# Expert stage of a hybrid decoder step: gathers of four slots for 32 tokens, a value sum in four column blocks, a key ring of six rows

## What is computed

```python
def peer_ffn(xn, w_q, keys1, keys2, u, v):          # 8 heads, 16 experts chosen per head
    q = (xt @ w_q).reshape(n, PEER_HEADS, 2, PEER_HALF)
    s1, s2 = einsum(q[:, :, 0], keys1), einsum(q[:, :, 1], keys2)
    v1, i1 = lax.top_k(s1, 16); v2, i2 = lax.top_k(s2, 16)
    cand = v1[..., :, None] + v2[..., None, :]
    top_s, sel = lax.top_k(cand, 16)                # idx = i1 * 128 + i2 of the chosen
    g = jax.nn.softmax(top_s)
    act = gelu(einsum('pd,ped->pe', xb, u[idx]))    # a dot product with each gathered key row
    return einsum('pe,ped->pd', g * act, v[idx])    # weighted sum of the gathered value rows
```

## Time and profile before

| | |
|---|---|
| median of 3 runs | 4652.41 us (4647.03 to 4680.39) |
| span of the profiled execution | 4664.4 us |
| expert stage in it, from the first key gather | 1476.6 us to the end |
| busy: PE, DVE, ACT, GpSimd | 3850.8, 2478.5, 1078.6, 2471.3 us |
| gathers | 2,176 of 0.524 MB |
| time from a gather's issue to its landing (median) | 6.3 us |

### The profile page before, as it was taken

One profiled execution on the slowest core, in us unless ns is written; L12 is line 12 of the kernel. 1 busy time (PEld: TensorE's weight loads), 2 busy tenths in 40 slices (PEclk: granted clock), 3 DMA queues, 4 the chain that ended last, 5 costly groups with the idle time before them and its releaser, 6 DMA issues.

```text
span 4664.4 us, 46976 instructions
## 1 busy us (share of the span) xinstructions
PE 3850.8 (83%) x13480; PEld 2174.6 (47%) x13480; DVE 2478.5 (53%) x6136; ACT 1078.6 (23%) x2482; POOL 2471.3 (53%) x2212
## 2 busy tenths in 40 slices
PE   8999997899884878787887787787788787878787
PEld 7888885555442334343343343343334343434332
DVE  3111004655434666666666666666666666666665
ACT  4221113333210212212222212222222121212221
POOL 0000000000002777777777777777777777777766
PEclk9999997999967999898999898989898999898989
DMA  3222214221136999999999999999999999999988
GB/s 135 89 85 99 77 41 155 75 65 46 53 100 252 369 379 350 385 368 362 368 375 371 367 382 363 360 373 361 358 389 352 363 374 364 346 374 358 361 322 309
DMA packets 393667, 1291.38 MB, mean 277 GB/s; under 512 B 48440, under 2 KB 84536, under 8 KB 391368
## 3 DMA queue, kind: packets, MB, share of 16 engines
q0 software_dynamic: 313920, 1143.22, 65.1%
q1 hardware_dynamic: 61080, 116.93, 7.4%
q10 hardware_dynamic: 18432, 28.42, 1.7%
HBM read 1243.87 MB, written 45.71 MB: 276 GB/s over the span
## 4 chain that ended last, share of the span: by engine, by line
PE 30%; DVE 14%; DMA 12%; issue 8%; POOL 3%; ACT 2%; POOLq 0%; ACTq 0%; DVEq 0%; SPq 0%
PE e_o_ps L1776 24%; DMA e_u_rows<-in_u,e_expert 8%; PE e_q_ps L1744 4%; DMA e_v_rows<-in_v,e_expert 3%; POOL e_v_rows L1429 2%; POOL e_u_rows L1429 1%; DVE e_pairs L1583 1%; DVE e_pairs L1608 1%; DVE e_top_idx L1585 1%; DVE e_top_idx L1582 1%; DVE e_pairs L1612 1%; DVE e_picked L1614 1%; DVE e_top_val L1584 1%; DVE e_pos L1585 1%; PE e_w_ps L1731 1%
## 5 line engine op out<-in xcount | busy, mean ns | idle before, releaser
L1776 PE MATMUL e_o_ps<-e_v_rows,e_diag 128*128 128x512 f32 (+1 forms) x4352 | 2061.4, 626 | 380.7 <-ACT e_diag L1499 289.3
L1631 DVE CUSTOM_DVE_ANT_0 e_u_rows<-e_u_rows,e_xn 128x1024 f32<-128x1024 f32 x1088 | 1300.6, 1223 | 1058.0 <-DMA e_u_rows<-in_u,e_expert 974.5
L1776 PEld LDWEIGHTS e_o_ps<-e_v_rows,e_diag 128*128 128x128 f32 (+1 forms) x4352 | 828.9, 197 | 1464.2 <-issue 1375.3
L1429 POOL DMA_INDIRECT e_v_rows<-in_v,e_expert x1024 | 1177.2, 1150 | 351.1 <-issue 250.8
L1429 POOL DMA_INDIRECT e_u_rows<-in_u,e_expert x1024 | 1114.3, 1088 | 376.4 <-issue 268.7
L1499 ACT ACTIVATE e_diag<-e_ident,e_weight 128x128 f32<-128x128 f32 x1024 | 361.9, 395 | 872.9 <-PE e_o_ps L1776 869.4
L1744 PEld LDWEIGHTS e_q_ps<-e_xnT,e_wq 128*128 128x128 f32 x2304 | 307.7, 209 | 117.9 <-issue 109.2
L1744 PE MATMUL e_q_ps<-e_xnT,e_wq 128*128 128x128 f32 x2304 | 314.4, 294 | 40.3 <-issue 34.0
L578 POOL TENSOR_TENSOR p_gate<-p_gate,gn 128x1024 f32<-128x1024 f32 x8 | 18.9, 2357 | 448.9 <-DMA p_gate<-z_tok 448.9
L373 PE MATMUL j_m<-j_wh,j_xh 128*128 128x512 f32 (+1 forms) x648 | 248.0, 383 | 4.5 <-DVE j_wl L309 2.5
L374 PE MATMUL j_m<-j_wl,j_xh 128*128 128x512 f32 (+1 forms) x648 | 246.2, 380 | 0.0
(11 more groups left out here) (255 smaller groups left out, 3930.1 us busy)
## 6 DMA issues: line engine op xcount, KB each, us to landing
j_w<-in_w_big SPq DMA_DIRECT2D x12, 2048.0 KB, 8.1
z_tok<-j_stage ACTq DMA_DIRECT2D x64, 256.0 KB, 2.0
e_u_rows<-in_u,e_expert POOLq DMA_INDIRECT x1024, 6.3
e_v_rows<-in_v,e_expert POOLq DMA_INDIRECT x1024, 6.3
z_feat<-j_stage ACTq DMA_DIRECT2D x32, 256.0 KB, 2.0
e_wq<-in_wq SPq DMA_DIRECT2D x2, 4096.0 KB, 24.0
e_room<-merged SPq DMA_DIRECT2D x9, 512.0 KB, 6.6
e_h_next<-in_x SPq DMA_DIRECT2D x9, 512.0 KB, 9.3
```

Of the source, the lines that this page charges most:

```text
L1429: pool.indirect_dma_start(ring[:, k % size, :], None, table, bass.IndirectOffsetOnAxis(ap=index[:, h % IDX, k:k + 1], axis=0)).then_inc(go ...
L1631: dve.tensor_tensor_reduce(u_rows[:, k % U_RING, :], u_rows[:, k % U_RING, :], xn[:, :], 1.0, 0.0, ALU.mult, ALU.add, dots[:, h % 2, k:k + ...
L1776: last = pe.matmul(o_ps[0:n, c * BANK:(c + 1) * BANK], diag[:, k % DIAGS, 0:n], v_rows[:, k % V_RING, c * BANK:(c + 1) * BANK], start=Fals ...
```

## The change

- A gather no longer fetches slot k of 128 tokens, but four slots of 32 tokens: partition 32 s + p holds slot 4 s + g of token 32 j + p. A full unit still has 16 gathers of 128 rows (j, g = 0 to 3), in the last tile 8.
- For this the chosen experts and their gates must move between partitions. DVE writes the expert numbers as floats beside the exponentials (`chosen`), `soften` divides by the sum ahead of the spreading, PE multiplies with a constant 0/1 matrix (`spreading`, four small products), and ACT copies the parts into `row4` (expert numbers) and `gate4` (`respread`, eight copies).
- A reduction needs token 32 j + p in partition 32 s + p, so `xn` goes to DRAM once a tile (`keep_xn`) and comes back four times over, in 16 loads of 32 rows (`load_x4`), a block j as soon as the last unit of the tile before has done with it. `take` goes.
- The weights of a gather are placed by `stack`, a 128 x 32 matrix of four identities one above the other. The value sum of one g is four products of 32 columns each, in the four column blocks of PE's array, for each half of the width. A value slot is freed after the whole group (`group_end`), not one by one.
- The key ring has 6 rows, the value ring still 8; the diagonals have 16 buffers of 32 columns.
- The loops over tiles are written out in full; constants come from DRAM rather than from GpSimd.

```diff
-    U_RING, V_RING = 8, 8
+    U_RING, V_RING = 6, 8
...
-        xn = sb("e_xn", [P, D])
+        x4 = sb("e_x4", [P, 4, D])
-        diag = sb("e_diag", [P, DIAGS, P])
+        diag = sb("e_diag", [P, TOPK, QUAD])
+        spread_ps = t_ps[1][:, 0, :].rearrange("p (j x) -> p j x", j=4)
...
+            def keep_xn(t):
+                wait_alone(sp, xn_ready, t + 1, tick)
+                sp.dma_start(xn_dram[t, :, :], xn_next[:, :]).then_inc(xn_out, 16)
+            def load_x4(t):
+                wait_alone(sp, xn_out, 16 * (t + 1), tick)
+                for j in range(quads(t)):
+                    if t:
+                        wait_alone(sp, u_used, before(t * HEADS - 1) + 4 * (j + 1), tick)
+                    wait_alone(sp, x4_in, 64 * (4 * t + j), tick)
+                    for s in range(4):
+                        sp.dma_start(x4[s * QUAD:(s + 1) * QUAD, j, :],
+                                     xn_dram[t, j * QUAD:(j + 1) * QUAD, :]).then_inc(x4_in, 16)
...
+            def u_gather(unit, q):
+                seq, n = before(unit) + q, quads(unit // HEADS)
+                column = q % 4 * n + q // 4
+                wait_alone(pool, u_used, seq - U_RING + 1, tick)
+                pool.indirect_dma_start(u_rows[:, seq % U_RING, :], None, u_dram,
+                                        bass.IndirectOffsetOnAxis(ap=row4[:, unit % IDX, column:column + 1], axis=0)
+                                        ).then_inc(u_got[seq % U_RING], 16)
+            def v_gather(unit, k):
+                seq = before(unit) + k
+                if seq >= V_RING:
+                    wait_alone(pool, v_used, group_end(seq - V_RING), tick)
...
+            for unit in range(UNITS):
+                pool.wait_ge(row4_ready, unit + 1)
...
+            def respread(unit):
+                b, n = unit % IDX, quads(unit // HEADS)
+                act.wait_ge(spread_done, unit + 1)
+                wait(act, v_used, 4 * (unit - IDX + 1))
+                for s in range(4):
+                    quad = slice(s * QUAD, (s + 1) * QUAD)
+                    act.activation(gate4[quad, b, 0:4 * n].rearrange("p (g j) -> p j g", j=n),
+                                   spread_ps[quad, 0:n, TOPK + 4 * s:TOPK + 4 * s + 4], ACT.Copy)
+                    last = act.activation(row4[quad, b, 0:4 * n].rearrange("p (g j) -> p j g", j=n),
+                                          spread_ps[quad, 0:n, 4 * s:4 * s + 4], ACT.Copy)
+                last.then_inc(row4_ready, 1)
...
-                    act.activation(diag[:, k % DIAGS, 0:eye.shape[1]], eye[:, :], ACT.Copy,
-                                   scale=weight[:, h % 2, k:k + 1]).then_inc(diag_ready, 1)
+                    act.activation(diag[:, k, :], stack[:, :], ACT.Copy,
+                                   scale=weight[:, unit % 2, k:k + 1]).then_inc(diag_ready, 1)
...
+            def soften(unit):
+                b = unit % IDX
+                dve.wait_ge(e_done, unit + 1)
+                chain.link(dve.reciprocal(e_rec[:, b:b + 1], e_sum[:, b:b + 1]))
+                dve.tensor_scalar(chosen[:, b, TOPK:], chosen[:, b, TOPK:], e_rec[:, b:b + 1], None,
+                                  ALU.mult).then_inc(chosen_ready, 1)
...
+            select(0)
+            select(1)
+            soften(0)
+            for unit in range(UNITS):
+                t, h = divmod(unit, HEADS)
+                if unit + 1 < UNITS:
+                    soften(unit + 1)
...
+                u_dots(unit)
+                if unit + 2 < UNITS:
+                    select(unit + 2)
+                weights(unit)
...
+            def spreading(unit):
+                pe.wait_ge(chosen_ready, unit + 1)
+                wait(pe, row4_ready, unit)
+                pe.wait_ge(xnT_ready, 2 * (unit // HEADS + 1))
+                for j in range(quads(unit // HEADS)):
+                    last = pe.matmul(spread_ps[:, j, :], spread[:, j, :], chosen[:, unit % IDX, :], start=True, stop=True)
+                last.then_inc(spread_done, 1)
...
+            def v_sum(unit, g):
+                n = quads(unit // HEADS)
+                final = unit % HEADS == HEADS - 1 and g == 3
+                pe.wait_ge(diag_ready, before(unit) + (g + 1) * n)
+                for j in range(n):
+                    seq = before(unit) + g * n + j
+                    pe.wait_ge(v_got[seq % V_RING], 16 * (seq // V_RING + 1))
+                for c in range(D // BANK):
+                    for j in range(n):
+                        last = pe.matmul(o_ps[j * QUAD:(j + 1) * QUAD, c * BANK:(c + 1) * BANK],
+                                         diag[:, g * n + j, :],
+                                         v_rows[:, (before(unit) + g * n + j) % V_RING, c * BANK:(c + 1) * BANK],
+                                         start=False, stop=final)
+                last.then_inc(v_used, 1)
...
+                if unit + 1 < UNITS:
+                    spreading(unit + 1)
```

More of the change, by code:

```diff
@@ L1392, in _ @@
                     sp.dma_start(keys[:, :, :], keys_dram).then_inc(keys_in, 16)
+            keep_xn(0)
+            load_x4(0)
             sp.dma_start(g_final[:, :], g_final_dram.to_broadcast([P, D])).then_inc(consts, 16)
-            def tile(t):
-                if not (isinstance(t, int) and t == 0):
+            for t in range(LAST + 1):
+                if t:
                     store(t - 1)
-                if not (isinstance(t, int) and t == LAST):
+                if t < LAST:
                     load_x(t + 1)
                     load_merge(t + 1)
-            tile(0)
-            with sp.Fori(1, LAST) as t:
-                tile(t)
-            tile(LAST)
+                    keep_xn(t + 1)
+                    load_x4(t + 1)
             store(LAST)
@@ L1456, in _ @@
-            tile(0)
-            with pool.Fori(1, LAST) as t:
-                tile(t)
-            tile(LAST)
-            for k in range(slots(LAST)):
-                v_gather(LAST, HEADS - 1, k)
+            def u_gather(unit, q):
[5 more added lines that the diff above has]
+                                        ).then_inc(u_got[seq % U_RING], 16)
@@ L1463, in _ @@
+            for k in range(4 * quads(LAST)):
+                v_gather(UNITS - 1, k)
         @block.scalar
@@ L1647, in weights, with u_dots @@
-                if slots(t, h) == TOPK:
-                    product(0, P, 0, 1, TOPK).then_inc(w_ready, 1)
-                else:
-                    chain.step(product(0, NSAMP, 0, 2, TOPK // 2))
-                    product(NSAMP, P, 1, 2, TOPK // 2).then_inc(w_ready, 1)
+                dve.tensor_scalar(chosen[:, b, TOPK:], chosen[:, b, TOPK:], e_rec[:, b:b + 1], None,
+                                  ALU.mult).then_inc(chosen_ready, 1)
+            def u_dots(unit):
+                t, h = divmod(unit, HEADS)
+                wait(dve, gelu_done, unit - 1)
+                n = quads(t)
+                for q in range(4 * n):
+                    seq, (j, g) = before(unit) + q, divmod(q, 4)
+                    if h == 0 and g == 0:
+                        dve.wait_ge(x4_in, 64 * (4 * t + j + 1))
+                    dve.wait_ge(u_got[seq % U_RING], 16 * (seq // U_RING + 1))
+                    dve.tensor_tensor_reduce(u_rows[:, seq % U_RING, :], u_rows[:, seq % U_RING, :], x4[:, j, :], 1.0, 0.0,
+                                             ALU.mult, ALU.add,
+                                             dots[:, unit % 2, g * n + j:g * n + j + 1]).then_inc(u_used, 1)
@@ L1653, in out_mean, with weights @@
+            def weights(unit):
+                n = 4 * quads(unit // HEADS)
+                dve.wait_ge(gelu_done, unit + 1)
+                wait(dve, diag_ready, before(unit - 1) if unit else 0)
+                dve.tensor_tensor(weight[:, unit % 2, 0:n], gelus[:, unit % 2, 0:n], gate4[:, unit % IDX, 0:n],
+                                  ALU.mult).then_inc(w_ready, 1)
             def out_mean(t):
@@ L1668, in _ @@
             dve.wait_ge(norm_in, 16)
[L1669 removed]
+            dve.wait_ge(layout_in, 64)
             for c in range(2):
@@ L1672, in _ @@
             norm(0)
[L1673 to L1707 removed]
+            select(0)
+            select(1)
+            soften(0)
+            for unit in range(UNITS):
+                t, h = divmod(unit, HEADS)
+                if unit + 1 < UNITS:
+                    soften(unit + 1)
+                if h == 1 and t:
+                    out_mean(t - 1)
+                if h in RESIDUAL and t < LAST:
+                    residual(t + 1, RESIDUAL.index(h))
+                if h == HEADS - 2 and t < LAST:
+                    norm(t + 1)
+                u_dots(unit)
+                if unit + 2 < UNITS:
+                    select(unit + 2)
+                weights(unit)
+                if h == 1 and t:
+                    out_norm(t - 1)
             out_mean(LAST)
@@ L1734, in w_out, with query @@
                     last.then_inc(wo_done, 1)
-            def query(unit, h, t, half):
```

(4 more changed lines are left out.)

326 lines of the change are left out of this document (112 added, 214 removed).

## The result

The changed kernel takes 4824.27 us (median of 4 runs, 4810.91 to 4829.21), against 4662.01 us of the kernel before on the same chip: the ratio is 1.0333, 95% interval 1.0297 to 1.0370. It is 3.3% slower; forecast were 2.4% and 4762 us. The kernel before was measured anew beside the experiments and took 4662 to 4679 us (medians), so where two experiments are compared, their ratios to it say more than their medians. The profiled execution has a span of 4820.8 us, 156.4 more than the 4664.4 of before.

The account below looks back on a forecast made before the run. GpSimd's gather issue was taken as the bound; 81 + 13 + 11 - 17 - 2 + 16 + 8 = +110 on the 4664.4 us span gives 4774, predicted as 4762 us because that span lies 12 above the median; range 4630 to 4880.

Parts of the forecast that it names:

- What bounds the kernel: Expert stage: GpSimd's gather issue, slowed by DVE's reductions, sets 46.3 us a unit; a quicker value sum buys almost nothing.
- Key ring of 6: Seventh key gather waits for DVE's first reduction; 46.75 us a unit, 382 a tile, +81 us for seven tiles (17 to 151).
- 0.45 for spreading: Unit start on DVE: small operations spreading the choice delay the first reduction, +0.45 us a unit.
- The ring's step that failed: Head 6: with the loop closed, DVE's pause for the norm counts in full, 4.2 us a tile.
- x4: Head 7: the normalised rows' loads hold up key gathers, 2 us a tile, 16 us in all (0 to 55).
- The value sum in blocks: PE: four column blocks overlap, a group takes 3.4 us and costs nothing, except 8 us in all at heads 4 and 1.
- the mark of 6.4: PE: time in us the unit's first value-sum group may take before value gathers must wait for it.
- (b): Rival: column blocks run one after another and PE becomes the bound; +432 us, 5194 us; chance 0.15.
- Start, tile 0, end: First gather waits for both selects and spreading, +11 us; tile 0's ring loss +13; end after the last units -2.
- Last tile: Six units of 8 slots run as a closed loop of 24.0 us each, 144 for 161.4: -17 us (-25 to -5).
- (a): Rival: the smaller ring hides, GpSimd stays the bound and the kernel gets faster; -60, 4592 us; chance 0.14.
- (c): Rival: nothing to measure, ring at its lower bound, x4 and PE cost nothing; -1, 4651 us; chance 0.16.

Follow-up runs that it names:

- half_values: Kernel before with only the first half of the columns of each value sum computed; 4664.91 us, ratio 0.9979.
- psum_x: Kernel before, loops written out, with the normalised tile that the key reductions read in PSUM, not SBUF; 4441.56 us, ratio 0.9506.
- ring6: Kernel before, loops written out, with the key ring cut from 8 rows to 6; 4751.73 us, ratio 1.0185.
- ring8: Changed kernel with a key ring of 8 rows, half the query weights loaded and used twice to make room; 4749.37 us, ratio 1.0175.
- no_x4: Changed kernel without the loads of normalised rows for tiles 1 to 8, reducing against tile 0's rows; 4795.25 us, ratio 1.0262.
- norm_first: Changed kernel with the next tile's norm (square and root) ahead of the eight spread copies on ACT at head 6; 4791.51 us, ratio 1.0249.
- all_three: Changed kernel with 8 key-ring rows, the norm ahead of the spread copies, and no normalised-row loads for tiles 1 to 8; 4688.89 us, ratio 1.0042.
- unrolled: Kernel before with its tile loops written out on all five engines, nothing else; 4663.33 us, ratio 0.9993.
- one_block: Changed kernel with all value-sum products but those of each tile's final group written into the same 32 columns; 5052.63 us, ratio 1.0819.

## Why the prediction was right, and where it was short

**What bounds the kernel**: right. PE could lose half its value sum for nothing (`half_values`), and GpSimd's issue, held up by the reductions, set the unit: without the hold it falls from 46.3 to 43.1 us (`psum_x`). The limit of the transfers behind it was put at 40.9 us a unit, which no kernel reached.

**Key ring of 6**: right in place, nearly in size. The wait before the seventh key gather is in all 56 units of tiles 1 to 7. Counted from a unit's first reduction, the seventh, eighth, ninth and sixteenth key gathers go at 2.0, 5.8, 9.3 and 29.0 us (medians) where 2.3, 6.9, 10.0 and 29.2 were forecast, and the sixteenth reduction is at 35.3 for 35.1: the first steps come sooner, and the unit is as long all the same. The ring alone costs 88 us (`ring6`), undone 75 (`ring8`). Without the 0.45 for spreading the forecast is 378.5 us a tile; `ring6` has 381.0. The agreement of the 382 with what is left of the changed kernel's tile is partly luck: 390.8, less 4.8 (`no_x4`: 386.0) and 4.4 (`norm_first`: 386.4), is 381.6, but `ring6` and the 4.8 that `all_three` leaves over `unrolled` make 385.8. The 5.5 us a tile that were booked as a gain from the loops were none (`unrolled`); the 11.6 did not rest on them, since they came from a closed loop's length against 370.5.

**The ring's step that failed** is the one on the norm at head 6. The prediction took its length, 4.2 us, from the kernel before, which fits a short ring alone (51.1 us in `ring6` where 51.0 were forecast), and had named the small copies of ACT, but only as covered by PE's half query. What it left out is what stands behind them on ACT: the square that DVE waits for. Asking on ACT too what is queued behind the copies, and who waits for that, would have given it from the diff. Forecast from head 5's first reduction to head 6's were 46.75 + 4.2 = 51.0 us, measured 54.7, and 50.0 with the square first.

**x4**: the mechanism was right (the loads fall into head 7, landing rises from 5.2 to 8.6 us), the size too small: 2 us a tile counted as one gather's delay of 1.28 us and something, measured 4.8, 29 to 33 us in all for 16. The prediction itself had named a landing of 7 us and more as what would take it higher.

**The value sum in blocks**: right. 3.46 us for a group after a pause (granted clock 0.55 over it), 3.4 forecast, under the mark of 6.4. The 8 us booked for heads 4 and 1 were not tried alone. Above the mark, at 7.05 to 9.76 (`one_block`), it costs 228 us. The rival (b) had asked 432 for that, too much: it reckoned every group at the length after a pause, 9.8 us, while in `one_block` two groups of three take some 7.05 us, and the granted clock is 0.87 to 0.88 in the three stretches from 2200 to 3700. The rule of the Trainium skill's "TensorE: Matmul & The Clock Gate", Part 3, by which weight loads overlap only where the row group differs (the same part also allows for a load into a background buffer), costs nothing that shows: 16 products with their loads, all on the same rows, take 3.46 us at the lower clock, a quarter of what twice 7.05 would be.

**Start, tile 0, end**: +10.4 up to the first reduction, where some +9 were forecast and 2 more in the first unit, and -3.3 for -2 at the end. Tile 0 was forecast at 16 and 6 us short; it has the norm and the x4 loads of the others.

**Last tile**: -3.5 for -17. The closed loop of 24.0 us holds for heads 2 to 5 (23.1 to 24.5), but heads 0 and 1 took 33.2 and 29.4 (36.9 and 31.0 in the kernel before). Head 0 has 8 key gathers and the 16 value gathers of the unit before it. What DVE waits for between head 0's last reduction and head 1's first, 20.1 us instead of the 10.6 of heads 2 to 5, are the scores and ScalarE's square for `out_mean`, 9.3 us together (changed kernel, order of time):

```profile
4623.28 0.42 DVE L1579 COPY e_s_sb<-e_s_ps 128x256 f32<-128x256 f32 x1 [5.69 <-PE e_s_ps L1724]
...
4637.59 0.15 DVE L1639 TENSOR_SCALAR e_stat<-e_stat 128x1 f32<-128x1 f32 x1 [3.62 <-ACT e_room L1511]
```

In the kernel's order PE does the scores behind the second group of the value sum, and the square needs the last group; the second and the last group stood 5.2 and 5.8 us waiting for value rows. So it is the previous unit's full value sum that holds the short unit up, which the prediction, with one length for six units, left out. What head 1 loses was not looked into.

**The rivals**: (a) was ruled out by `ring6`, (c) by the time. (b) did not come, but `one_block` shows that it was a real one.

## What to carry to other kernels

Before speeding an engine up, ask what taking its work away would change; a page that shows it 83% busy does not tell, and here the answer was nothing, while the two ring rows that paid for it were worth 75 to 88 us. Where a buffer ring closes a loop between two engines, go through the queue of every engine that the loop runs through, at each place where something else is interleaved (a norm, a load), since a pause there can reach the issuing engine. And look for what holds up the issuing engine: one operand moved to PSUM made the kernel 5% faster where the whole change made it 3% slower, and two ring rows were worth as much as before (89 us for 88).

## What the runs showed that had not been expected

- A reduction whose second operand lies in PSUM takes as long as with both in SBUF (1,218 against 1,223 ns), and the mean gather holds GpSimd 0.95 us for 1.12.
- A ring two rows short costs 89 us also where the transfers show a busy share of 1.00; in the stretch shown the share did not move, the rate fell from 395 to 387 GB/s. A share of DMA engines near 1 is no proof that nothing upstream counts.
- Products of 32 columns cost 0.44 us each on one block of columns at the full clock, like full-width ones, and 0.22 at the lower clock on four.
